# Decoder step with mLSTM and sparse attention: the first two score groups and their exponentials placed inside the compression run

## What is computed

```python
hid = jax.nn.gelu(jnp.einsum('bnlgd,lde->bnge', blocks, w1))
return jnp.einsum('bnge,ef->bngf', hid, w2)
...
p_c = masked_softmax(jnp.einsum('bqgrd,bngd->bgrqn', qp, kc) * scale, cmp_end[None, :] <= qpos[:, None])
...
p_s = masked_softmax(jnp.einsum('bqgrd,bgqnd->bgrqn', qr, ks) * scale, (tok <= qpos[:, None])[:, :, None])
...
p_w = masked_softmax(jnp.einsum('bqgrd,bkgd->bgrqk', qr, kw) * scale, mask_w)
```

## Time and profile before

| | |
|---|---|
| median of 3 runs | 2086.28 us (2083.65 to 2087.95) |
| the profiled execution's own time | 2083.28 us |
| its span, first to last instruction | 2081.4 us |
| mean granted TensorE clock | 0.956 of full speed |
| PE busy | 1964.0 us (94%) |
| DVE busy | 979.3 us (47%) |
| ACT busy | 672.9 us (32%) |

### The profile page before, as it was taken

How to read it: one execution, slowest core, us unless ns; L and a number is a source line. 1 busy time by engine, 2 the same in 40 slices (tenths; PEclk the granted TensorE clock), 3 DMA queues, 4 the chain that set the end, 5 groups by cost and what they waited for, 6 DMA issues and landing times. The chain is left out here.

```text
span 2081.4 us, 34572 instructions
## 1 busy us (share of the span) xinstructions
PE 1964.0 (94%) x14490; PEld 1784.9 (86%) x14490; DVE 979.3 (47%) x1696; ACT 672.9 (32%) x1315; POOL 107.6 (5%) x148
## 2 busy tenths in 40 slices
PE   6999988889999999999989999888899999999997
PEld 5877865569999999999977788655799999999996
DVE  6334656733355442444363256566333555424434
ACT  4523236742223221222234222466322332212221
POOL 0021221000000000000001122200000000000000
PEclk9989988989999999999999899889899999999998
DMA  4202352012222223222131122610222222222221
GB/s 180 101 31 67 102 161 84 1 53 91 91 82 92 84 89 105 83 90 92 62 114 41 41 77 92 194 41 4 78 84 92 87 87 92 82 92 90 83 92 44
DMA packets 47531, 174.18 MB, mean 84 GB/s; under 512 B 6442, under 2 KB 6474, under 8 KB 46930
## 3 DMA queue, kind: packets, MB, share of 16 engines
q1 hardware_dynamic: 40178, 142.71, 21.3%
q0 software_dynamic: 7200, 29.27, 4.2%
HBM read 161.37 MB, written 14.71 MB: 85 GB/s over the span
## 5 line engine op out<-in xcount | busy, mean ns | idle before, releaser
L835 PE MATMUL ps<-xh,late_w 128*128 128x272 f32 x3840 | 645.3, 289 | 1.8 <-ACT slab L1508 1.8
L835 PEld LDWEIGHTS ps<-xh,late_w 128*128 128x128 f32 x3840 | 544.7, 189 | 2.5 <-issue 2.3
L1614 DVE TENSOR_TENSOR late_w<-ring,late_w 128x1024 fp32r<-128x1024 f32 x196 | 240.2, 1225 | 644.4 <-ACT late_w L1307 644.4
L1307 ACT CAST late_w<-ring 128x1024 fp32r<-128x1024 f32 x196 | 205.3, 1047 | 716.3 <-PE ps L835 716.2
L835 PE MATMUL ps<-xl,late_w 128*128 128x272 f32 x1920 | 397.4, 288 | 0.0
L835 PEld LDWEIGHTS ps<-xl,late_w 128*128 128x128 f32 x1920 | 303.2, 189 | 0.0
L835 PE MATMUL ps<-ah,late_w 128*128 128x272 f32 x1408 | 234.7, 288 | 0.0
L835 PEld LDWEIGHTS ps<-ah,late_w 128*128 128x128 f32 x1408 | 198.7, 188 | 0.0
L1481 ACT ACTIVATE slab<-ps,stat 128x31 f32<-128x31 f32 (+5 forms) x204 | 84.6, 451 | 81.3 <-DVE stat L1872 81.2
L835 PE MATMUL ps<-mh,late_w 128*128 128x272 f32 x576 | 98.8, 288 | 0.0
L1102 PE MATMUL ps<-const,slab 128*128 128x128 f32 (+1 forms) x384 | 63.5, 308 | 25.4 <-ACT slab L1491 25.4
(11 more groups left out here) (329 smaller groups left out, 2967.9 us busy)
## 6 DMA issues: line engine op xcount, KB each, us to landing
ring<-in_W SPq DMA_DIRECT2D x258, 512.0 KB, 3.4
slab<-in_pages POOLq DMA_DIRECT2D x64, 128.0 KB, 2.5
slab<-in_c POOLq DMA_DIRECT2D x8, 512.0 KB, 4.4
out_sC<-slab POOLq DMA_DIRECT2D x8, 512.0 KB, 3.0
slab<-in_win POOLq DMA_DIRECT2D x2, 2048.0 KB, 8.0
out_oldwin<-in_cwin POOLq DMA_DIRECT2D x2, 2016.0 KB, 13.4
xT<-in_xT SPq DMA_DIRECT2D x8, 272.0 KB, 4.6
out_y<-slab SPq DMA_DIRECT2D x8, 272.0 KB, 2.1
```

The lines of the kernel that those rows point to most:

```text
L835: mm = pe.matmul(out[:, a, :], w[:, k * P:(k + 1) * P], x[:, a * NHALF:(a + 1) * NHALF], start=start, stop=stop)
L1307: act.copy(hi, ring[:, u % RING, 0:hi.shape[1]]).then_inc(wh_ready, 1)
L1614: dve.tensor_tensor(lo, ring[:, u % RING, 0:hi.shape[1]], hi.bitcast(F32), ALU.subtract).then_inc(wl_ready, 1)
```

## The change

PE makes the scores of steps 0 and 1 before the last weight unit of the second compression run, not behind it. ACT takes the exponentials of both steps before the bias copies and the Gelu, not behind the copies of the second layer's results. Both hold in each of the two layers.

```diff
@@ -1214,13 +1214,14 @@
             compress(1, (0, 1))
             head_scales(2)
             head_scales(3)
-            compress(1, (2, 3))
+            compress(1, (2,))
 
             pe.wait_ge(rope_ready, since(layer, rope_ready, 6))
             pe.wait_ge(q_moved, since(layer, q_moved, 1))
             pe.wait_ge(ha_ready, since(layer, ha_ready, MH))
             att_scores(0)
             att_scores(1)
+            compress(1, (3,))
             w2 = sml("w2", "p (v f) -> p v f", v=2)
             pe.wait_ge(hid_ready, since(layer, hid_ready, 1))
             for g in range(NKV):
@@ -1509,6 +1510,8 @@
             act.wait_ge(ha_ready, since(layer, ha_ready, MH))
+            att_exp(0)
+            att_exp(1)
             for v in range(2):
                 act.wait_ge(w1_used, since(layer, w1_used, 4 * (v + 1)))
                 link(act.copy(hbias[:, v:v + 1], ps[:, HIDDEN_BANK[v][0], NBLK:NBLK + 1]))
@@ -1521,8 +1524,6 @@
             act.copy(gall[:, :, :], ps[:, 5, 2 * P:4 * P].rearrange("p (a n) -> p a n", a=2)[:, :, 0:3 * NH])
             act.copy(vcs, ps[:, 5, P:2 * P]).then_inc(cmp_ready, 1)
 
-            att_exp(0)
-            att_exp(1)
             att_scale(0)
```

## The result

| | before | changed |
|---|---|---|
| median of 19 runs, us | 2086.28 | 2099.86 |
| lowest to highest, us | 2083.40 to 2098.56 | 2098.36 to 2107.12 |
| profiled execution, us (span) | 2083.28 (2081.4) | 2105.8 (2104.1) |

The account below looks back on a forecast made before the run. It took the attention's head, a chain of turns between DVE, ACT and PE, as on the path. Scaling 5.5 us later a layer, 2 x 5.5 = 11, on the median 2086.28 gave 2097.3, stated as 2097; range 2091 to 2102.

Parts of the forecast that it names:

- The copies of queries hold the mask: Attention head, DVE: 16 query copies last to 292.28, so the earlier scores buy 1.27 us, not 2.1.
- The load stands behind the wait: Attention head, ACT: Exp's table loads only after the wait for DVE's maxima; first exponential 1.30 us after the load starts.
- The second layer at the lower clock: Behind the Gelu, PE: after over 5 us of rest, products to ACT's copies take 3.3 us instead of 1.84.
- Copies to scaling: Attention head: from ACT's copies to step 0's scaling 2.2 us in place of 4.76, the exponentials being done.
- The third load is hidden: ACT ahead of step 2: a 1.28 us table load fits in the 1.94 us wait for DVE and costs nothing.
- Sum: Whole kernel: step 0's scaling 5.5 us later in each of two layers, 11 us in all.
- whatever moves the start of that scaling moves the rest of the layer: Attention behind step 0's scaling: its end moves by as much as the scaling, 5.5 us a layer.
- the clock costs more: Rival: the later attention meets one more stretch at the lower clock, 2 us a layer, 2101; chance 0.10.
- the clock doesn't stay up: Denies the rival that PE's second layer keeps the full clock: 4.0 us a layer, 2094.3; chance 0.13.
- the load waits: Denies the rival that idle ACT loads Exp's table at once: 1.30 us less a layer, 2094.7; chance 0.05.
- the delay isn't absorbed: Denies the rival that something later in the layer, starting no earlier anyhow, absorbs the delay: no change, 2086; chance 0.05.
- the overlap doesn't work as drawn: Denies the rival that exponentials, loads and first Gelu lie beside the last unit: 1.4 us earlier a layer, 2083.5; chance 0.02.

Follow-up runs that it names:

- 38 copies: Kernel before with 38 added one-column copies a layer on ACT ahead of step 0's exponentials, to an unused tile, as plain delay: 2094.49 us, 1.0035.
- PE's split alone: Kernel before with only PE's new order, scores of steps 0 and 1 ahead of the last compression unit; exponentials in their old place: 2091.73 us, 1.0022.
- ACT's half alone: Kernel before with only ACT's exponentials of steps 0 and 1 moved ahead of bias copies and Gelu, PE as it was: 2101.18 us, 1.0066.
- the faster version: Kernel before with step 0's exponentials behind the Gelu, four rounding copies ahead of the bias copies, DVE's subtractions behind step 2's maxima: 2081.3 us, 0.9972.

## Why the prediction was right, and what it sized wrongly

The mechanism came out as predicted, step by step. With the anchor's 5.30 us taken off the rows after (predicted in brackets): first mask 292.33 (292.28), maxima end 293.75 (293.70), load 293.83 (293.74), first exponential 295.13 (295.04), bias copy 297.88 (297.79), first Gelu 299.39 (299.26), second layer's products 300.89 (300.9), copies 303.91 (304.2), scaling 305.99 (306.4). The head is 5.11 us later, not 5.5; the same in layer 1.

*The copies of queries hold the mask*: right, and shown by moving them (0.85 us earlier a layer).

*The load stands behind the wait*: right, and shown by taking it away (1.30 us a layer). By the drain of about 1.38 us that the Trainium skill, ScalarE: Activation LUTs, section What ACT_TABLE_LOAD costs, puts on each load, that would have been some 2.7. The trace disagrees: the bias copy ends at 303.38, the load starts at 303.40 and the Gelu at 304.69.

*The second layer at the lower clock*: right in kind, and shown by filling the rest (clock 1.00, wait 1.90 instead of 3.08). The term of 3.3 us from the products to the copies measured 3.02, so the factor is 1.6 and not the 1.8 of pure transposes. I take it, without having shown it, that part of the 1.84 is not PE's own time.

*Copies to scaling* 2.08, for a predicted 2.2. *The third load is hidden*: right; step 2's exponentials start 5.40 us behind the scaling, before 5.42, and still wait for DVE.

*Sum*: 2 x 5.11 = 10.2 for a predicted 11. The measured loss is 13.6 by the medians. That the forecast of 2097 comes within 3 us of 2099.86 is partly luck: it had the heads 0.8 us too long and put what lies behind them at nothing, where 3.4 us were measured, so the two misses partly cancel. The mis-sized term is the one at nothing: "whatever moves the start of that scaling moves the rest of the layer", by the same amount. The attentions behind it are 0.7 us longer a layer in both traces, which with the heads makes 11.6. What makes them longer wasn't isolated: the clock is low at other places (0.50 where it was 0.99), but in all for hardly longer, and with the table loaded ahead of the wait the attention of layer 0 has 52.4 us at 0.50 and yet its length of before (144.55). Nor does a later head bring it by itself: the kernels with that table load and with 38 copies have heads 3.8 and 3.5 later than before, and attentions of 144.6 and 144.7. The other 2 us I put in the parts behind, where the rival *the clock costs more* came in, at another place than I gave it: not in the attention alone but at the turn of the layers. Both traces of the changed kernel show the long stretch and tail, 5 to 6 us together, and both of these executions lie above the median. Only some of the executions can have them: from the anchor on these two traces take 1812.4 us, with the earliest anchor of all 14 traces (286.4) that is a span of 2098.8, and 11 of the changed kernel's 19 executions have a shorter one (2096.3 to 2098.1).

The other rivals fall: the clock doesn't stay up, the load waits, the delay isn't absorbed (the 38 copies cost 7.3 us for their own 7.0), and the overlap doesn't work as drawn. ACT's order alone gives the loss. The kernel with PE's split alone costs some 5 us, of which its trace shows 3.0 in the heads, half of it by the clock in layer 0; the split's cost isn't simply additive with ACT's, since under ACT's new order the earlier scores help.

The two lengths of the stretch are the clock's: in all 14 traces the norm's sums at the turn take 2.15 us where the stretch is long and 1.15 or 1.16 where it is short, and the mean granted clock over the ten microseconds from their start is 0.50 and 0.66. Open: why the clock falls earlier in one trace than in another. Kernels with a later head have either length (ACT's half alone 868.16, the change 872.58), and so do those with a shorter one (the faster version 868.05, step 0's exponentials behind the Gelu 872.73).

## What to carry to other kernels

Work that moves into an engine's idle time is free only up to the semaphore it waits for; whatever stands behind that wait in program order, a table load included, moves with it, so look at when the input of the moved work is ready, not at how long the engine is idle. In ACT's idle time ahead of the Gelu, rounding copies whose input comes during it, together with DVE's subtractions moved back, gained 5 us, and exponentials that had to wait for DVE's maxima lost 14. Compare the edited stretch against an anchor ahead of it, since the total of a long program hides two microseconds a layer.

## What was not expected of the hardware

The parts behind the edit have two lengths, 867.9 to 868.3 or 872.5 to 872.8 us for the stretch and 608.1 to 608.4 or 609.3 to 610.2 for the tail, at the same code and work. The time up to the first anchor ranges from 286.4 to 292.1 us in 14 traces, without relation to the kernel. All three go with the granted clock. The nine short stretches have 36.9 to 37.4 us at 0.50 and the five long ones 48.5 to 48.7; the six short tails have 14.2 to 14.5 and the eight long ones 18.8 to 19.6; the two shortest starts have 27.3 and the six longest 37.5. So the same code takes up to 6 us more or less by where the clock falls. A delay of 3.5 us in all and one of 7.0 cost 6.7 and 7.3, and a head 4.3 us shorter in all gained nothing that can be measured.
